# The scan's readout product in four column groups, with four transfers a round and the output products ahead of it in banks of their own

## The reference, cut to what matters

```
lam_bar = exp(lam * dt)
b_bar   = ((lam_bar - 1) / lam) * B
bu      = einsum('blgh,gph->blgp', u, b_bar)
states  = associative_scan(a_r * b_l + b_r over (lam_bar, bu))
y       = einsum('blgp,ghp->blgh', states, C).real     # both directions, summed
y      += d_skip * u
```

## Time and profile before

| | us |
|---|---|
| median of 3 runs | 1863.85 (1862.78, 1863.85, 1872.2) |
| the profiled execution | 1866.43 |
| its span | 1864.7 |
| TensorE matmuls busy | 1688.1 |
| VectorE busy | 706.2 |
| readout loop of layer 0, rounds 1 to 8 | 196 to 312 |
| readout loop of layer 1, rounds 1 to 8 | 1261 to 1356 |

### The profile page before, as it was taken

The page is one execution under the profiler, slowest core; times in us unless marked ns, Lnnn a source line. Parts: engine busy times, 40 slices in busy tenths (PEclk is TensorE's granted clock), DMA queues, the critical chain, the costliest instruction groups (busy, mean ns, idle before and its releaser), DMA issues.

```text
span 1864.7 us, 28853 instructions
## 1 busy us (share of the span) xinstructions
PE 1688.1 (91%) x11470; PEld 1024.0 (55%) x11470; DVE 706.2 (38%) x1564; ACT 418.5 (22%) x866; POOL 303.9 (16%) x263
## 2 busy tenths in 40 slices
PE   5999998989999999899988988998889999996697
PEld 2467555554444443456545556676557888453354
DVE  4578764650110112311101158696763111421123
ACT  4011112551000001322222250111144001331133
POOL 0004342770000000200000020045464000000000
PEclk9999998899999999999999989999889999997899
DMA  9311469219222153499999633125661346899981
GB/s 392 125 46 30 143 228 344 47 46 348 103 96 84 68 225 130 174 369 356 386 392 393 229 115 113 46 74 199 219 121 55 150 176 241 344 401 411 411 350 59
DMA packets 108139, 384.07 MB, mean 206 GB/s; under 512 B 42016, under 2 KB 61472, under 8 KB 68864
## 3 DMA queue, kind: packets, MB, share of 16 engines
q1 hardware_dynamic: 61040, 329.14, 45.6%
q10 hardware_dynamic: 42720, 22.72, 5.4%
q0 software_dynamic: 4272, 30.67, 4.8%
HBM read 363.09 MB, written 31.98 MB: 212 GB/s over the span
## 4 chain that ended last, share of the span: by engine, by line
PE 63%; DVE 12%; DMA 8%; SPq 6%; POOL 4%; issue 3%; ACT 3%; ACTq 1%; POOLq 0%; DVEq 0%
PE tile_ps L599 55%; SPq L535 6%; PE turn_ps L599 4%; DMA arena<-sorted_in 3%; POOL arena L2007 2%; DMA vn<-in_wpack 2%; PE out_ps L599 1%; DMA ring<-in_wpack 1%; PE turn_ps L920 1%; DVE arena L1870 1%; DMA x<-in_xT 1%; DMA arena<-in_rpb 1%; DVE smx L1852 1%; DVE arena L1515 1%; DVE arena L1562 1%
## 5 line engine op out<-in xcount | busy, mean ns | idle before, releaser
L599 PE MATMUL tile_ps<-h,ring 128*128 128x512 f32 (+1 forms) x1312 | 472.0, 514 | 6.7 <-ACT h L1130 5.0
L599 PEld LDWEIGHTS tile_ps<-h,ring 128*128 128x128 f32 x1312 | 250.0, 192 | 211.1 <-issue 195.5
L599 PE MATMUL tile_ps<-arena 128*32 128x256 f32 (+5 forms) x3152 | 270.1, 351 | 25.6 <-POOL arena L1997 5.8
L599 PE MATMUL tile_ps<-arena,ring 128*128 128x512 f32 (+1 forms) x704 | 235.3, 486 | 2.7 <-issue 2.7
L599 PEld LDWEIGHTS tile_ps<-arena 128*32 128x32 f32 (+4 forms) x3152 | 180.7, 140 | 84.0 <-issue 41.8
L599 PEld LDWEIGHTS tile_ps<-arena,ring 128*128 128x128 f32 x704 | 133.6, 190 | 96.6 <-issue 87.6
L2007 POOL TENSOR_SCALAR arena<-arena,smx 128x512 f32<-128x512 f32 (+1 forms) x96 | 129.1, 1362 | 74.0 <-DVE smx L1858 73.6
L599 PE MATMUL tile_ps<-ring,arena 128*32 128x256 f32 (+2 forms) x1008 | 95.9, 428 | 20.9 <-DMA ring<-in_wpack 14.4
L1344 ACT ACTIVATE arena<-tile_ps 128x512 f32<-128x512 f32 (+1 forms) x56 | 27.5, 491 | 347.3 <-PE tile_ps L599 347.3
L1891 DVE TENSOR_TENSOR arena<-tile_ps,arena 128x512 f32<-128x512 f32 (+1 forms) x32 | 17.9, 558 | 212.2 <-PE tile_ps L599 212.2
L599 PEld LDWEIGHTS tile_ps<-ring,arena 128*32 128x32 f32 (+1 forms) x1008 | 49.8, 125 | 57.2 <-issue 41.1
(11 more groups left out here) (316 smaller groups left out, 2272.0 us busy)
## 6 DMA issues: line engine op xcount, KB each, us to landing
ring<-in_wpack SPq DMA_DIRECT2D x176, 1024.0 KB, 7.6
arena<-in_wpack SPq DMA_DIRECT2D x64, 1024.0 KB, 16.0
h<-in_wpack SPq DMA_DIRECT2D x15, 1024.0 KB, 24.8
qa<-in_wpack SPq DMA_DIRECT2D x12, 1024.0 KB, 9.2
qn<-in_wpack SPq DMA_DIRECT2D x12, 1024.0 KB, 12.4
kn<-in_wpack SPq DMA_DIRECT2D x12, 1024.0 KB, 14.5
vn<-in_wpack SPq DMA_DIRECT2D x12, 1024.0 KB, 16.6
sorted_out<-arena ACTq DMA_DIRECT2D x44, 128.0 KB, 7.7
```

Of the source, the lines that this page charges most:

```text
L599: return nc.tensor.matmul(out, lhsT, rhs, start=start, stop=stop)
```

## The change

The readout product writes group g to partitions 32g to 32g+15, in 128 columns of its bank, and loops over the parts outside the groups. `zs` has 128 partitions x 15 lags of 16. One transfer a group, with `lag_rows`, takes all eight lags of a group at once, so `tm`'s rows are ordered by channel and then step; two of the four are on SP. For that order the state matrices, the input and the skip term are laid out anew. The output products go to `out_ps`, counted by `y_full` and `y_free`, and stand ahead of the readout product in TensorE's order.

```diff
-ON_SP = 4
+ON_SP = 2
@@ tile_jobs
-            out = [(l, "y", q - 1), (l, "yb", q - 1)] if q else []
-            names += out + late if q < NQ else late + out
+            names += late
@@ layout
-        dsk, a0 = cut(a0, [NGRP, GRP], parts=GRP)
+        dsk, a0 = cut(a0, [NQ, GRP])
-        wm, a1 = cut(a1, [2, GQ, STEP, GRP])
+        wm, a1 = cut(a1, [2, GQ, GRP, STEP])
-        zs, _ = cut(SSM["bre"].start, [GQ, (2 * STEP - 1) * GRP], parts=GRP)
+        zs, _ = cut(SSM["bre"].start, [(2 * STEP - 1) * GRP])
+        def lag_rows(g):
+            v = zs[32 * g:32 * g + GRP, 0:P]
+            (step, n), (one, m) = v.ap
+            return bass.AP(tensor=v.tensor, offset=v.offset, ap=[[step, n], [GRP, STEP], [one, m]])
@@ SP (and the same on ScalarE, for g in range(GQ - ON_SP))
                     if q >= 2:
-                        wait_full(sp, (l, "y", q - 2))
-                    for j in range(STEP - ON_SP, STEP):
-                        a = (STEP - 1 - j) * GRP
-                        sp.dma_start(tm[j * GRP:(j + 1) * GRP, q % 2], zs[:, :, a:a + P]).then_inc(tm_in, 16)
+                        sp.wait_ge(y_full, l * NQ + q - 1)
+                    for g in range(GQ - ON_SP, GQ):
+                        sp.dma_start(tm[:, q % 2, g], lag_rows(g)).then_inc(tm_in, 16)
@@ TensorE
                 for q in range(NQ + 1):
+                    if q == NQ:
+                        late_modulation(q)
+                    if q:
+                        o = q - 1
+                        fwd, bwd = out_ps[:, 0, :], out_ps[:, 1, :]
+                        if l * NQ + o:
+                            pe.wait_ge(y_free, l * NQ + o)
+                        pe.wait_ge(tm_in, 16 * GQ * (l * NQ + o + 1))
+                        pe.wait_ge(carried, l * NQ + o + 1)
+                        (the 24 calls as before, into fwd and bwd)
+                        b.then_inc(y_full, 1)
                     if q < NQ:
                         pe.wait_ge(cp_done, l * NQ + q + 1)
...
-                        for g in range(GQ):
-                            for r in range(2):
+                        for r in range(2):
+                            for g in range(GQ):
-                                    ins = mm(bank((l, "z", q, n))[0:GRP, g * P:(g + 1) * P], bb[d, r, q * GQ + g, :],
+                                    ins = mm(bank((l, "z", q, n))[32 * g:32 * g + GRP, 0:P], bb[d, r, q * GQ + g, :],
...
+                pe.wait_ge(y_free, (l + 1) * NQ)          (ahead of attention)
@@ ScalarE
-                act.dma_start(ug, u_dram.rearrange("j t (a g) c -> (j t a) g c", g=NGRP)).then_inc(ug_in, 16)
+                act.dma_start(ug, u_dram.rearrange("j t (a g) c -> (t a) j (g c)", g=NGRP)).then_inc(ug_in, 16)
@@ VectorE, readout_rows
-                back = bank(job)[0:GRP].rearrange("p (g n) -> p g n", g=GQ)
+                back = bank(job)[:, 0:P]
-                CP(zs[:, :, 0:(STEP - 1) * GRP], back[:, :, 0:(STEP - 1) * GRP]).then_inc(zd_done, 1)
+                CP(zs[:, 0:(STEP - 1) * GRP], back[:, 0:(STEP - 1) * GRP]).then_inc(zd_done, 1)
@@ VectorE, input and state matrices
-                    free(job, CP(up[:, m].rearrange("p (j c) -> p j c", j=STEP),
+                    free(job, CP(up[:, m].rearrange("p (j c) -> p j c", j=STEP)[:, ::-1],
-                    pv = [spread(pww[:, r, :, gs].rearrange("p j g -> p g j"), 3, GRP) for r in range(2)]
-                    bv = [spread(bb[:, r, gs, :], 2, STEP) for r in range(2)]
+                    pv = [spread(pww[:, r, :, gs].rearrange("p j g -> p g j"), 2, GRP) for r in range(2)]
+                    bv = [spread(bb[:, r, gs, :], 3, STEP) for r in range(2)]
@@ VectorE, output sum
-                        wait_full(dve, fwd)
-                        wait_full(dve, bwd)
-                        free(bwd, CP(v, bank(bwd)[:, 0:GQ * NCH]))
-                        wait_taken(dve, bwd)
-                        free(fwd, TT(v, v, bank(fwd)[:, 0:GQ * NCH], ALU.add))
+                        dve.wait_ge(y_full, l * NQ + o + 1)
+                        link(CP(v, out_ps[:, 1, 0:GQ * NCH]))
+                        TT(v, v, out_ps[:, 0, 0:GQ * NCH], ALU.add).then_inc(y_free, 1)
@@ GpSimd
-                        wait_full(pool, (l, "yb", q - 2))
-                        wait_full(pool, (l, "y", q - 2))
+                        pool.wait_ge(y_full, l * NQ + q - 1)
```

More of the change, by code:

```diff
@@ L436, in backbone @@
         wm_done, carried = sem("wm_done"), sem("carried")
+        y_full, y_free = sem("y_full"), sem("y_free")
         trig_in, trig_out = sem("trig_in"), sem("trig_out")
@@ L850, in _ @@
                             wait_bank(pe, (l, "z", q, n))
-                        for g in range(GQ):
-                            at_q = (q % 2) * GQ + g
-                            for r in range(2):
+                        for r in range(2):
+                            for g in range(GQ):
+                                at_q = (q % 2) * GQ + g
                                 for n, (d, lags) in enumerate(((lower, slice(0, STEP)), (upper, slice(2, NPOS)))):
-                                    ins = mm(bank((l, "z", q, n))[0:GRP, g * P:(g + 1) * P], bb[d, r, q * GQ + g, :],
+                                    ins = mm(bank((l, "z", q, n))[32 * g:32 * g + GRP, 0:P], bb[d, r, q * GQ + g, :],
                                              cp[d, r, at_q, lags].rearrange("p a b -> p (a b)"), r == 0, r == 1)
@@ L858, in _ @@
                                         full((l, "z", q, n), ins)
[L859 to L866, removed]
-                        pe.wait_ge(carried, l * NQ + o + 1)
-                        for g in range(GQ):
-                            G = o * GQ + g
-                            cols = slice(g * NCH, (g + 1) * NCH)
-                            for d, to in ((lower, fwd), (upper, bwd)):
-                                mm(bank(to)[:, cols], tm[d, o % 2, g, :], ug[d, G, :], True, False)
-                            for r in range(2):
-                                co = cp[:, r, (o % 2) * GQ + g, 1:STEP + 1].rearrange("p a b -> p (a b)")
-                                f = mm(bank(fwd)[:, cols], co[lower], st[lower, 0:STEP, r, G].rearrange("p j b -> p b j"), False, r == 1)
-                                s = st[upper, 0:STEP, r, G].rearrange("p j (a b) -> p a b j", a=2)[:, :, ::-1, ::-1]
-                                b = mm(bank(bwd)[:, cols], co[upper], s, False, r == 1)
-                        full(fwd, f)
-                        full(bwd, b)
                     if 0 < q < NQ:
@@ L898, in _ @@
                 us = pairs[l]
+                pe.wait_ge(y_free, (l + 1) * NQ)
                 pe.wait_ge(rope_done, (l + 1) * (KW + 1))
@@ L1266, in _ @@
                         if q:
-                            act.wait_ge(tm_in, 16 * STEP * (l * NQ + q))
+                            act.wait_ge(tm_in, 16 * GQ * (l * NQ + q))
                         job = (l, "z", q, 0)
-                        copy(job, zs[:, :, (STEP - 1) * GRP:], bank(job)[0:GRP].rearrange("p (g n) -> p g n", g=GQ))
+                        copy(job, zs[:, (STEP - 1) * GRP:], bank(job)[:, 0:P])
                         act.wait_ge(zd_done, 2 * (l * NQ + q + 1))
                         if q >= 2:
-                            wait_full(act, (l, "y", q - 2))
-                        for j in range(STEP - ON_SP):
-                            a = (STEP - 1 - j) * GRP
-                            act.dma_start(tm[j * GRP:(j + 1) * GRP, q % 2], zs[:, :, a:a + P]).then_inc(tm_in, 16)
+                            act.wait_ge(y_full, l * NQ + q - 1)
+                        for g in range(GQ - ON_SP):
+                            act.dma_start(tm[:, q % 2, g], lag_rows(g)).then_inc(tm_in, 16)
                     if q == NQ:
@@ L1289, in _ @@
                         copy_rows(l, MOD1 + q)
-                for q in range(NQ):
-                    wait_taken(act, (l, "y", q))
-                    wait_taken(act, (l, "yb", q))
+                act.wait_ge(y_free, (l + 1) * NQ)
                 act.dma_start(y_dram.rearrange("j t (a g) c -> (j t a) g c", g=NGRP), ug).then_inc(y_out, 16)
```

31 lines of the change are left out of this document (19 added, 12 removed).

## The result

The changed kernel takes 1882.97 us, the median of 7 runs (1877.46 to 1886.23); the kernel before, run beside it, 1867.54 (1862.78 to 1874.31). The ratio is 1.0073, 95% interval 1.0048 to 1.0099: slower, where 1834 us was forecast. The profiled execution took 1880.72 us, its span is 1879.0, 14.3 more than before.

What follows compares the result with a forecast made beforehand. TensorE, busy in 91% of the span, was taken as the bound. Layer 0's rounds gave 7.3 + 4.5 us, layer 1's 10.7 + 8.5, attention's start -0.6: 30.4 off the 1863.9 median, so 1834 us, range 1825 to 1850.

Steps and rivals of the forecast that it cites:

- The readout product: TensorE, each scan round: eight tiles abreast cut the product from 1.92 us to 0.6, a gain of 1.3 us a round.
- bank waits: Layer 0: TensorE's 0.57 us waits for a bank go, because output products leave `tile_ps`.
- Two abreast only: Rival, 15%: row halves and column groups don't combine, so all 1.3 us readout gains go; time 1846 us.
- The order: Output product starts at once in full rounds; GpSimd, released ahead of the readout product, has 11 us for its 8.9.
- The state matrices: VectorE's `wm` operations, reading powers at a step of 32: stay at 0.69 us, bounds 0.69 to 1.2; no cost taken.
- cover: VectorE idle time that can hide slower `wm` operations: about 3.2 us in five rounds a layer, none in two.
- The transfers: Eight issues become four, ScalarE and SP each free 1.3 us sooner; landing kept at 2.5 us, up to 6.3.
- The light rounds: Rounds 5 to 8, to attention: layer 0 gains 4.5 us, between 1 and 7.5; layer 1 gains 8.5.
- the second rival: 15%: light rounds get a new wait, for transfers just issued or VectorE's loop, and keep their lengths; 1847 us.
- the first step of the chain: Layer 1, rounds 5 to 8: from output product 4's start to product 5's start, 9.7 us, with landing 4.9.
- The clock: Named as a sign of being wrong: a lower granted clock stretches what is left; no size given.
- Kept or not: Forecast kept the loops' gains; rival, 5%: attention or the experts wait for what didn't move, 1862 us.

Runs made afterwards that it cites:

- e3: Changed kernel plus one wait: GpSimd starts its quarter only after VectorE has finished the round's readout rows; ratio 0.9999 to the kernel before, span 1866.1 us.
- e12: Changed kernel with the readout product ahead of the output products again and the powers table kept as [group, step], without GpSimd's wait; ratio 0.9974 to the kernel before.
- e5: The repaired kernel: changed kernel with the powers table kept as [group, step] and GpSimd waiting for VectorE's readout rows; ratio 0.9981 to the kernel before, span 1855.2 us.
- e2: Changed kernel with the powers table kept as [group, step], so state-matrix multiplications avoid the 32-element step; ratio 1.0040 to the kernel before, span 1870.0 us.
- e4: Kernel before with only the output products moved to `out_ps` and ahead of the readout product; ratio 1.0142 to the kernel before, span 1900.1 us.
- e8: Kernel before with output products in `out_ps` ahead of the readout product, and GpSimd waiting for VectorE's readout rows; ratio 1.0069 to the kernel before, span 1879.8 us.
- e10: e5 with useless TensorE products filling the wait before the sixth output products, 4 in layer 0, 7 in layer 1; ratio 0.9921 to the kernel before.
- e1: Changed kernel with the old order put back, readout product ahead of the previous round's output product; ratio 1.0055 to the kernel before, span 1877.3 us.
- e15: Changed kernel with 7 useless TensorE products ahead of layer 1's sixth output product; ratio 1.0084 to the kernel before.
- the best version: e10 with more useless products before layer 1's seventh and eighth output products and round 8's modulation in both layers; ratio 0.9904 to the kernel before, median 1851.2 us.

## Why the prediction was wrong

**The readout product**: right, 0.65 us for the 0.6 taken; eight abreast. The bank waits went. In layer 0's rounds 1 to 4 the repaired kernel gains 9.1 us where 7.3 was forecast. *Two abreast only* fell.

**The order**: the step that failed in the full rounds. The text says that GpSimd's start "moves ahead of z(q), and it has a whole round of 11 us for its 8.9". That counted GpSimd's own time and not what it does to VectorE while it runs, although the doubled operation had its row and was used for the light rounds. While GpSimd runs, VectorE's second half of `carry_in` takes 4.85 us in place of 1.47, and the rotary product and the transfers behind it come late. It turned a forecast gain of 18.0 us in the full rounds of both layers into a loss of 7.2. e3 gives 21 us of the full rounds back with one wait; they then gain 13.9 us of the 18.0. The Trainium skill, "SBUF — State Buffer", section "SBUF: two separate sides", has the rule that GpSimd and a VectorE operation with two SBUF inputs exclude each other; here the trace agrees, with 1.41 us in place of 0.39, while the addition at 210.29 that reads one of its inputs from PSUM keeps its 0.16 us beside GpSimd. What the order was to bring by itself, the end of the waits for GpSimd, came in the changed kernel, but e12, which leaves the order as before, has a ratio of 0.9974 against e5's 0.9981.

**The state matrices**: mis-sized. Taken at 0.69 us with an upper bound of 1.2; measured 1.03 for four of the six. The cover was as forecast in kind (11.9 us of idle are left in layer 1), yet the stages grew by 6.1 and 7.6 us. In layer 1 TensorE waits for L1784, 2.33 and 2.70 us, where it waited 0.96 and 1.88, and the stage's granted clock falls from 0.94 to 0.88; in layer 0 it waits once, 2.14 us. In e2, 2.7 and 7.0 us come back. By the prediction's own cover (3.2 us in five rounds, none in two) four operations at 1.03 would have cost 2 x 4 x 0.34 = 2.7 us a layer, an estimate: right for layer 0, too low for layer 1, where the clock is missing from it.

The 3.2 us that e2 leaves in layer 0's stage aren't the operations' doing. They are there too in e4 and e8 (116.0 us), which have `wm` as before. The traces of the kernel before and of e5 show the place, the same wait of the same length:

```profile
145.33 1.97 PE L599 MATMUL tile_ps<-arena 128*128 128x64 f32 x16 [1.42 <-ACT arena L1257]
```

```profile
145.44 3.64 PE L604 MATMUL tile_ps<-arena 128*128 128x64 f32 x16 [1.42 <-ACT arena L1262]
```

Before, TensorE stays at the higher level through the whole stage (granted clock 1.00, 112.7 us); so it does in e10 and e12. In e5 it runs at half speed behind the wait (0.97 for the stage, 115.9 us); so it does in the changed kernel (3.38 us there). e1 and e3 have two such stretches, one of them behind the 2.14 us for L1784 that left the changed kernel at full speed, and take 122.9. So a good half of what layer 0's stage lost is luck of the clock as far as these runs show: a wait of 1.42 us had half speed behind it in some kernels and not in others, and why is open.

**The transfers**: the landing times were kept because "as many bytes move". Median 2.8 and 2.7 us and a largest of 6.3 bear that out over all rounds, but not where the sum used it, as the light rounds show.

**The light rounds**: the second rival came true. Forecast 43.4 and 30.7 us; the repaired kernel has 46.4 and 42.0, before 47.9 and 39.0. In layer 0 the weights fit with it as forecast (DMA share 0.98, and 0.96 in the repaired kernel). In layer 1 the first step of the chain, 9.7 us, took 13.6 (1308.46 to 1322.02): the transfers were issued from 1314.6 on, 2.0 us later than reckoned, and the last landed after 6.7 us and not 4.9. The sum has a slip besides: "The same again: 26.7" adds 9.3 us to 17.4, where the step before it was 7.7, and the text names nothing for the 1.6 us more. The later steps are at half speed, which the sum doesn't have. With filler two of them take 8.0 and 11.3 us for the forecast 7.7 and 9.3.

**The clock**: named only as what could make the forecast wrong, and not priced. Behind gaps of 7 and 8 us TensorE's next 11.6 us (5.38, 1.08, 1.87, 3.30) run at half speed, and e10 shows that it is the waiting: the same round without a gap in TensorE's work runs at full speed. That a filled gap is not enough by itself is seen in e15, where TensorE was slow before it, and that a short wait doesn't always bring half speed in layer 0's `wm` stage. Repaired without filler is 0.9981, with filler 0.9904 to 0.9921.

**Kept or not**: forecast kept. Part of what a loop gains or loses is given back in the first 30 us of attention: 32.8 us before, 28.6 after, 35.0 in the repaired kernel (TensorE waits 4.64 us for ScalarE's L1313 there, 2.59 before). What holds ScalarE can be seen: its second issue of a bias transfer there (L1180, L1175 before) takes 5.23 us in the repaired kernel, 3.33 before and 0.62 in the changed one, where the first 18 us move 172 GB/s and not 281. That the earlier start runs into the weights there is likely, but no run tried it.

Of 30.4 us forecast, the best version brings about 18 (0.9904 of 1867.5). What remains open: how much of the 2.4 us ahead of layer 0's first `wm` operation is chance (e2, e3 and e5 start it within 0.4 us of before), and why the same short wait in layer 0's stage brings half speed in some kernels and not in others.

## What to carry to other kernels

When a product is moved ahead, list whom it releases, and lay the released engine's new stretch over what VectorE does then: GpSimd's start is worth a wait of its own. Price each new wait of TensorE twice, as the gap and as half speed that may follow it, and where a gap of several us can't be removed, try to fill it. Two repairs that the profile shows as stretched durations (a step of 32 elements, VectorE beside GpSimd) brought 23.8 us of span, from a changed kernel that had lost 14.3.

## What was not expected of the hardware

- A float32 VectorE operation of 128 x 512 with one operand read at a step of 32 elements takes 1.03 us when that step is inmost, 0.69 when it is one level out.
- Beside GpSimd the smallest operation suffers most: 16 columns in 0.93 us, at most 1.35, in place of 0.18.
- The same wait of 1.42 us in the same place was followed by full speed in some kernels (1.97 us for 16 instructions) and by half speed in others (3.64 us).
- Four transfers of 64 KB from one queue land up to 15.3 us after their issue under the weight loads, two from each of two queues up to 6.3 (changed kernel) or 8.6 (e5).
- Products of no use, 0.9 us each (14 instructions in 6.28 us), made the kernel faster.
